# A norm's factor multiplied in behind the mixing products, and half-height gate blocks paired on the tensor engine

## What is computed

```python
h = rms_norm(x, norm_mix[l])                 # x * rsqrt(mean(x*x) + EPS) * gain
proj = h @ w_in[l]
xr, yr, q, k, v, g_a, g_b = jnp.split(proj, IN_SPLITS, axis=-1)
u  = causal_depthwise_conv(xr, conv_w[l], conv_b[l])       # width 4
r  = sigmoid(block_diag_linear(u, w_a, b_a))               # 16 blocks of 88 x 88
i  = sigmoid(block_diag_linear(u, w_x, b_x))
hr = scan(exp(-8 r softplus(-lam)), sqrt(...) * i * u)
y_a = (gelu(yr) * hr) @ w_up_a[l]
y_b = chunked_attention(norm(q), norm(k), v) @ w_up_b[l]
x = x + (sigmoid(g_a + b) * y_a + sigmoid(g_b + b) * y_b) @ w_out[l]
```

## Time and profile before

| what | value |
|---|---|
| median of 3 runs | 2690.18 us |
| the profiled execution's own time | 2690.39 us |
| its span in the trace | 2688.6 us |
| PE busy | 2659.7 us (99%), 11968 matmuls |
| DVE, ACT, POOL busy | 838.9, 1128.5, 1138.0 us (31%, 42%, 42%) |
| mean granted clock of TensorE | 0.997 of full speed |
| DMA | 262 MB, 97 GB/s |

### The profile page before, as it was taken

The page is one execution under the profiler, slowest core; times in us unless marked ns, Lnnn a source line. Parts: engine busy times, 40 slices in busy tenths (PEclk is TensorE's granted clock), DMA queues, the critical chain, the costliest instruction groups (busy, mean ns, idle before and its releaser), DMA issues.

```text
span 2688.6 us, 31940 instructions
## 1 busy us (share of the span) xinstructions
PE 2659.7 (99%) x11968; PEld 2158.1 (80%) x11968; DVE 838.9 (31%) x1515; ACT 1128.5 (42%) x1647; POOL 1138.0 (42%) x484
## 2 busy tenths in 40 slices
PE   8999999999999999999999999999999999999999
PEld 7888878888876788888888888788888767888887
DVE  3223035551235333221132231446312453322200
ACT  5333234743546434333243332357435464433321
POOL 4444444445331334444444444444544313344443
PEclk9999999999999999999999999999999999999999
DMA  4333623333322333332333332233333232333322
GB/s 150 94 97 98 224 82 94 94 94 102 101 67 77 98 94 102 94 101 93 97 94 99 96 95 93 86 97 89 93 104 105 62 96 85 88 101 99 96 90 75
DMA packets 254657, 261.95 MB, mean 97 GB/s; under 512 B 8992, under 2 KB 241216, under 8 KB 254560
## 3 DMA queue, kind: packets, MB, share of 16 engines
q1 hardware_dynamic: 250064, 252.02, 31.5%
q10 hardware_dynamic: 4496, 8.57, 0.9%
HBM read 258.38 MB, written 10.57 MB: 100 GB/s over the span
## 4 chain that ended last, share of the span: by engine, by line
PE 40%; issue 39%; POOL 20%; POOLq 0%; DMA 0%; ACT 0%; SPq 0%; DVE 0%; ACTq 0%
POOL wlo L431 20%; PE ps L1183 11%; PE ps L1188 11%; PE ps L1187 11%; PE ps L1340 1%; PE ps L1398 1%; PE ps L1413 1%; PE ps L1357 1%; PE ps L1362 1%; PE ps L1361 1%; PE ps L1322 0%; PE ps L1321 0%; DMA raw<-in_w_gate 0%; POOLq L430 0%; POOLq L438 0%
## 5 line engine op out<-in xcount | busy, mean ns | idle before, releaser
L431 POOL TENSOR_TENSOR wlo<-raw,whi 128x1024 fp32r<-128x1024 f32 x472 | 1136.7, 2412 | 1529.2 <-ACT whi L472 1529.2
L1183 PE MATMUL ps<-h_lo,whi 128*128 128x512 f32 x2272 | 895.8, 394 | 14.6 <-DVE h_lo L795 7.6
L1188 PE MATMUL ps<-h_hi,wlo 128*128 128x512 f32 x2272 | 886.7, 390 | 0.0
L1187 PE MATMUL ps<-h_hi,whi 128*128 128x512 f32 x2272 | 886.7, 390 | 0.0
L472 ACT ACTIVATE whi<-raw 128x1024 fp32r<-128x1024 f32 x472 | 494.7, 1054 | 722.6 <-PE ps L1183 693.3
L1183 PEld LDWEIGHTS ps<-h_lo,whi 128*128 128x128 f32 x2272 | 427.9, 188 | 116.9 <-issue 17.4
L1188 PEld LDWEIGHTS ps<-h_hi,wlo 128*128 128x128 f32 x2272 | 427.8, 188 | 89.8
L1187 PEld LDWEIGHTS ps<-h_hi,whi 128*128 128x128 f32 x2272 | 428.1, 188 | 87.5 <-issue 1.0
L1183 PE MATMUL ps<-act_lo,whi 128*128 128x512 f32 x704 | 274.0, 389 | 0.0
L1188 PE MATMUL ps<-act_hi,wlo 128*128 128x512 f32 x704 | 273.9, 389 | 0.0
L1187 PE MATMUL ps<-act_hi,whi 128*128 128x512 f32 x704 | 273.9, 389 | 0.0
(11 more groups left out here) (160 smaller groups left out, 2643.4 us busy)
## 6 DMA issues: line engine op xcount, KB each, us to landing
raw<-in_w_in SPq DMA_DIRECT2D x124, 512.0 KB, 3.7
raw<-in_w_gate SPq DMA_DIRECT2D x88, 512.0 KB, 3.7
raw<-in_w_up SPq DMA_DIRECT2D x88, 512.0 KB, 3.7
raw<-in_w_down SPq DMA_DIRECT2D x80, 512.0 KB, 3.4
rel_band<-rel_rows ACTq DMA_DIRECT2D x1, 8192.0 KB, 39.1
raw<-in_w_up_b SPq DMA_DIRECT2D x16, 512.0 KB, 3.8
raw<-in_w_out SPq DMA_DIRECT2D x16, 512.0 KB, 3.3
raw<-in_rg_band SPq DMA_DIRECT2D x14, 512.0 KB, 3.5
```

The source lines that it names most:

```text
L431: nc.gpsimd.tensor_tensor(wlo[:, s, :], raw[:, s, :], whi[:, s, :].bitcast(F32), ALU.subtract).then_inc(lo_made, 1)
L1183: ins = pe.matmul(ps[:, b, :], w_hi, x_lo, start=start, stop=False)
L1187: pe.matmul(ps[:, b, :], w_hi, x_hi, start=False, stop=False)
L1188: return pe.matmul(ps[:, b, :], w_lo, x_hi, start=False, stop=stop)
```

## The change

The mixing stage treats the norm as the FFNs do. h is x times the gain, made by `renewed` behind FFN 1's down products; `norm` goes. The sum of squares (two parts instead of three) stands behind the first chunk of XR; ACT makes the factor into a buffer of its own, `rstd_mix`, after its second chunk copy. Every result of a product with h is multiplied by it when it leaves PSUM: XR into `tmp` (a new DVE instruction for each tile; the convolution now reads `tmp`, which has two tiles), YR and gate B (in place of copies), G (two tiles at t == 8 of DVE's loop over the recurrent branch's output, six behind it; ACT's sigmoid then reads SBUF), q and k (DVE, before ACT's squares, whose copy goes), and v (by position, so the factor is needed as a column: PE transposes `rstd_mix` behind the fifth chunk of XR, and DVE copies the column to `rstd_col`).

The second part: where a gate's result tile m has at most 64 rows from tile m-1 and at most 64 from tile m+1, the four neighbour blocks are packed into two (`rg_blocks`). A packed block holds the rows 64 to 127 for one gate and the rows 0 to 63 for the other, and is multiplied by six matmuls over 64 rows, in turn on the two halves, into two banks. That is so for m = 1, 3, 5, 7, 9: 52 blocks instead of 62, of which 10 are packed. A chunk holds 7 blocks instead of 8; there are 8 chunks for the gates as before. Before a packed block PE waits for the last packed one's matmuls (`halves_done`).

The 10 packed blocks of a layer have 60 matmuls over 64 rows, as many as the 20 full blocks that they replace. The core of the diff:

```diff
-BANDS = [(m, g, k) for m in range(KR) for g in range(2) for k in (m - 1, m, m + 1) if 0 <= k < KR]
-BPC = CW // P
+        if 0 < below <= HALF and 0 < above <= HALF:
+            blocks += [(m, [(0, m, 0, P)]), (m, [(0, m - 1, HALF, P), (1, m + 1, 0, HALF)]),
+                       (m, [(1, m, 0, P)]), (m, [(0, m + 1, 0, HALF), (1, m - 1, HALF, P)])]
+BPC = CW // P - 1
...
-                ffn(None, False, decay_begun, None if l else bands_made)
-                rstd_from(0)
-                for t in range(KD):
-                    hi_of(h_hi[:, t, :], tmp[:, t % 2, :])
+                ffn(lambda t: col("mix", t), False, decay_begun, None if l else bands_made)
...
+                        if t == 0:
+                            rstd_from(0, rstd_mix[:, :])
...
-                ffn(None, False, decays)
-                norm("mix")
+                ffn(lambda t: col("mix", t), False, decays)
...
+                def scaled(dst, b):
+                    dve.wait_ge(for_dve, C.next(for_dve))
+                    nc.vector.tensor_tensor(dst, ps[:, b, :], rstd_mix[:, :], ALU.mult
+                                            ).then_inc(bank_read[b], C.made(bank_read[b]))
...
-                            u[:, t, back:S], ps[:, b, 0:S - back], col("conv_w", (CONV - 1 - back) * KR + t),
+                            u[:, t, back:S], tmp[:, t % 2, 0:S - back], col("conv_w", (CONV - 1 - back) * KR + t),
...
+                    if t:
+                        dve.wait_ge(xr_used, C.now(xr_used))
+                    for n in both:
+                        scaled(tmp[:, n % 2, :], mix_bank(XR_T + n))
+                    if t == 2:
+                        dve.wait_ge(col_turned, C.next(col_turned))
+                        nc.vector.tensor_copy(rstd_col[:, :], ps[:, 1, 0:S:P]).then_inc(bank_read[1], C.made(bank_read[1]))
...
+                    if t == 8:
+                        ga_out(0)
+                        ga_out(1)
...
-                summed(0, [square[:, 1, :], tmp[:, 0, :], tmp[:, 1, :]])
+                def norm_behind(g):
+                    if g == 0:
+                        summed(0, [square[:, 0, :], square[:, 1, :]])
+                def columns_turned(g):
+                    if g == 0:
+                        pe.wait_ge(rstd_made, C.next(rstd_made))
+                        pe.wait_ge(bank_read[1], C.now(bank_read[1]))
+                        for n in range(KS):
+                            at = slice(n * P, (n + 1) * P)
+                            ins = pe.transpose(ps[:, 1, at], rstd_mix[:, at], ident[:, :])
...
+                    if len(parts) == 2:
+                        pe.wait_ge(halves_done, C.now(halves_done))
+                    at = slice(n % BPC * P, (n % BPC + 1) * P)
+                    for i, (w, u_) in enumerate(((whi, u_lo), (whi, u_hi), (wlo, u_hi))):
+                        for g, kk, r0, r1 in parts:
...
+                            ins = pe.matmul(ps[:, b, :], w[r0:r1, s, at], u_[r0:r1, kk, :],
+                                            start=i == 0 and n == rg_at(m, g)[0], stop=done)
```

More of the change, by code:

```diff
@@ L44, with rg_blocks, rg_at @@
 K0, V0, G0 = Q0 + D, Q0 + 2 * D, Q0 + 3 * D
-BANDS = [(m, g, k) for m in range(KR) for g in range(2) for k in (m - 1, m, m + 1) if 0 <= k < KR]
-BPC = CW // P
-RG_CHUNKS = -(-len(BANDS) // BPC)
+HALF = P // 2
+def rg_blocks():
+    blocks = []
+    for m in range(KR):
+        below, above = m * P % RB, -(m + 1) * P % RB
+        if 0 < below <= HALF and 0 < above <= HALF:
+            blocks += [(m, [(0, m, 0, P)]), (m, [(0, m - 1, HALF, P), (1, m + 1, 0, HALF)]),
+                       (m, [(1, m, 0, P)]), (m, [(0, m + 1, 0, HALF), (1, m - 1, HALF, P)])]
+        else:
+            blocks += [(m, [(g, k, 0, P)]) for g in range(2) for k in (m - 1, m, m + 1) if 0 <= k < KR]
+    return blocks
+BLOCKS = rg_blocks()
+BPC = CW // P - 1
+RG_CHUNKS = -(-len(BLOCKS) // BPC)
+def rg_at(m, g):
+    return [n for n, (of, parts) in enumerate(BLOCKS) if of == m and any(p[0] == g for p in parts)]
 G8 = [(0, 4), (4, 8)]
@@ L514, in renewed @@
                 act.wait_ge(bank_read[b], C.now(bank_read[b]))
[L515 to L523, removed]
+                high(t, x[:, t, :], gain)
+                squared(t, x[:, t, :])
             def ffn(gains, ends=False, first=None, behind=None):
@@ L623, in _ @@
                 conv_hi(KR - 1)
-                blocks = chunks = 0
+                chunks = 0
                 for m in range(KR):
                     for g in range(2):
-                        blocks += sum(b[:2] == (m, g) for b in BANDS)
-                        while chunks * BPC < blocks:
+                        while chunks * BPC <= rg_at(m, g)[-1]:
                             ring()
@@ L1291, in _ @@
                     if n % BPC == 0:
                         s = chunk()
[L1293 removed]
+                    while seen <= max(kk for _, kk, _, _ in parts):
                         pe.wait_ge(split_lo, C.next(split_lo))
                         seen += 1
[L1296 to L1300 removed]
@@ L1301, in _ @@
-                    ins = product(b, *columns(s, n % BPC * P, 0), u_hi[:, kk, :], u_lo[:, kk, :], first, last)
-                    if last:
-                        ins.then_inc(for_act, C.made(for_act))
-                        C.step(bank_read[b])
+                    for g, _, _, _ in parts:
+                        b = mix_bank(RG_T + 2 * m + g)
+                        if n == rg_at(m, g)[0]:
+                            pe.wait_ge(bank_read[b], C.now(bank_read[b]))
+                    if len(parts) == 2:
+                        pe.wait_ge(halves_done, C.now(halves_done))
```

133 lines of the change are left out of this document (67 added, 66 removed).

## The result

The changed kernel takes 2674.35 us (median of 4 runs, 2671.85 to 2675.09); the kernel before, on the same chip, 2690.84 (2689.87 to 2691.74). The ratio is 0.994, with a 95% interval of 0.9927 to 0.9952: faster by 16.5 us, where 18.2 were forecast. The profiled execution took 2675.09 us.

The account below looks back on a forecast made before the run. PE, busy 99% of the span, was taken to bound the kernel. Gains and losses of 16.4 + 5.6 - 2.0 - 1.8 = 18.2 us took the median from 2690.18 to 2672.0 us; the 8-in-10 range was 2663 to 2681.

Parts of the forecast that it names:

- The norm, +16.4 us: At the mixing stage's norm: 21.6 us lost over both layers taken as removed, 5.2 put back, 16.4 us gained.
- shorter second wait: At the norm ahead of the mixing stage: PE waits 3.6 us for h_lo in each layer, with a shorter wait behind.
- The sum of squares: Inside XR's stream, in two parts: costs PE 1.72 us per layer; the last square just arrives in time for its second half.
- The transposes: Four transposes of the factor on PE in XR: 0.88 us per layer, read from a group in the attention loop.
- The packed blocks, +5.6 us: In RG: a packed block costs 1.08 us and replaces two blocks of 1.36 us together; 20 of them save 5.6 us.
- The scores: Attention's float32 matmuls on two row halves, taken as the packed blocks' pattern: halves at once, 0.40 us lost entering and leaving.
- The free switch: In RG's packed blocks: no loss on entering and leaving, a bound of 13.6 us saved; no separate chance given.
- the halves one after the other: Rival in RG: the two row halves don't run at once, so packing only costs, 8.0 us; about 2686 us, chance 0.07.
- the float32 rate: Rival in RG: 64-row matmuls run at float32 speed, a packed block 2.98 us, 32.4 us more; 2710 us, chance 0.03.
- the 0.05 us: Sign in RG that the forecast is right: the halves of a packed block start within 0.05 us of each other.
- RG's start, -2.0 us: A convolution lengthened by POOL ends the first sigmoid 11.3 us after RG's start; PE waits about 1.0 us more per layer.
- G, -1.8 us: In G: two `ga_out` multiplications on DVE lengthen PE's 1.43 us chunk wait by 0.9 us per layer, between 0 and 1.4.

Follow-up runs that it names:

- Experiment 5: The changed kernel with DVE multiplying XR tiles by the factor in place in PSUM, where ACT and the convolution read them: 2675.0 us (2671.53 to 2675.15).
- experiment 1: The changed kernel with the gates' blocks as before, so only the norm's part is left: 2677.38 us, ratio 0.995 to the kernel before.
- Experiment 4: The changed kernel with one of ACT's two chunk copies behind G's first sigmoids moved ahead of them into the recurrent branch: 2667.7 us, ratio 0.9912.
- experiment 3: The changed kernel with a packed block's three matmuls of one half written ahead of the other half's three, instead of in turn: 2675.48 us (one run).
- 7: The changed kernel with the two packed blocks of a result tile next to each other (full, full, packed, packed): 2673.94 us, ratio 0.9937.
- experiment 8: The changed kernel with each XR tile's convolution right behind its multiplication, instead of both multiplications of a pair first: 2688.26 us (one run).

## Why the prediction was right, and where it wasn't

The time forecast was 2672.0 us and it is 2674.35, in the range of 2663 to 2681. Step by step:
- **The norm, +16.4 us: right.** The trace gives 17.1. (The shorter second wait that the prediction read in each layer stood in layer 1 alone, 0.36 us; the sum doesn't use it.) The sum of squares costs 1.72 us as forecast, and its second half never waits for the last square. The transposes were put at 0.88 us, by the group of eight matmuls in the earlier trace rows; here the group has four and costs 0.44, 0.9 us more for both layers. Alone, this part brings 13.4 us by the medians: in its trace 3.1 us go against it from YR to UA, the low clock of one layer included, and 0.5 in RG.
- **The packed blocks, +5.6 us: a little high.** 1.10 us a block against 1.08; RG without a wait is 39.70 us, 4.9 us less in both layers. The scores were the right row to read the price of the switch from. The free switch (2664) is refuted by 0.42 us a block, the halves one after the other and the float32 rate by the same 1.10 us. The halves of a packed block start 1 to 14 ns apart, inside the 0.05 us that the prediction named. The Trainium skill's model (TensorE: Matmul & The Clock Gate, section Measured speedup vs the span model) would have given the free switch. Its 4 ns for a further tile agree with the 3 or 4 ns between most starts here, but it has no term for going in and out of packed matmuls, and these rows have 0.42 us.
- **RG's start, -2.0 us: right.** The sigmoid started 10.2 us after RG's start and ended after 10.9 (forecast 10.6 and 11.3), and the wait costs 0.74 us a layer instead of 1.0. The forecast had 2.3 + 2.4 + 2.3 = 7.0 us for the two convolutions and a POOL subtraction between them; the six taps took 6.69, one of them 2.9. Experiment 5 shows the cause by taking it away: with PSUM as one input the taps are 746 ns whatever POOL does. By the Trainium skill, SBUF — State Buffer, section Who interferes with whom, it is the second SBUF input that contends; the taps of 2.9 us, against none over 0.751 in experiment 5, agree.
- **G, -1.8 us: the step that failed.** The place was right and the wait of 2.15 us close to the 2.3 named; experiment 1 puts it down to the norm's part, and the copy's 0.72 us fit the cause, DVE's added work. The price wasn't: 2.30 and 2.38 us a layer against 0.9. The step took the cost of a longer wait to be its length. Of the 2.3 us some 0.7 are the wait; 1.64 are the clock, which fell to the 1.2 GHz level behind it. Inside its stream the kernel before showed half clock only at the norm, behind 3.6 us, and none behind 1.43 us in G, and I priced nothing in between. Experiment 4 removed both parts with one copy.

The terms as measured are 17.1 + 4.9 - 1.5 - 4.7 = 15.8 us, against the 15.3 of the two profiled executions. That the norm came out 0.7 us better and the packing 0.7 us worse than forecast, so that the two cancel, is luck.

What stays open: why a wait of 2.1 to 2.2 us in G is sometimes followed by the low clock and sometimes not. It was in both layers of the change and of experiments 3 and 7, in layer 0 alone with the norm's part alone, in layer 1 alone in experiment 8, and in neither layer in the profiled run of experiment 5. The length doesn't decide it within these: the eight waits with it were 2.12 to 2.17 us, the four without it too. I made no run that varies the length of the wait by itself.

## What to carry to other kernels

Where a stage's wait is made longer, even by less than a microsecond, look for the granted clock behind it: here 0.7 us more of wait took 1.64 us with it in most traces, and moving one copy ahead of a table load, into time in which its engine idled, gave back 6.65 us. When an elementwise factor moves behind a product, multiply it in place in PSUM if the reader would otherwise get a second SBUF operand while POOL works. And two parts of a change are not independent merely because they touch different engines: the faster gates made the late sigmoid dearer.

## What the hardware showed that I had not expected

- Two matmuls on different row halves start together although two others stand between them in the program (experiment 3: 1.10 us a block either way).
- Packed blocks pay for going in and out: 0.42 us a block, and the scores in plain float32 had 0.40.
- The clock fell to 1.2 GHz for about 3.4 us behind a wait of only 2.15 us, inside a stream that was otherwise full, and didn't behind 2.17 us in experiment 1's layer 1.
- One tap with both tensor inputs in SBUF took up to 2.9 us instead of 0.75 when it met a POOL subtraction, and a tile's three taps 3.26 and 4.33 us instead of 2.3 (experiment 8), while with PSUM as one input they kept their 746 ns each (experiment 5).
